# A decoder layer with 32 experts on one core: gate and up of the next expert ahead of each down, a direct gather for the first group, and one and a half weight units more loaded ahead

## What is computed

```python
def hier_moe(h, w_rg, b_rg, w_re, b_re, w_gate, w_up, w_down):
    ...
    lg = xf @ w_rg.astype(jnp.float32) + b_rg.astype(jnp.float32)
    pg = jax.nn.softmax(lg, axis=-1)
    g_star = jnp.argmax(lg, axis=-1)
    ...
    pe = jax.nn.softmax(le, axis=-1)
    top_p, top_i = lax.top_k(pe, TOP_K)
    w = p_group * top_p / jnp.sum(top_p, axis=-1, keepdims=True)
    e_idx = g_star[:, None].astype(jnp.int32) * EXPERTS_PER_GROUP + top_i.astype(jnp.int32)
    y = grouped_experts(x, e_idx, w.astype(x.dtype), w_gate, w_up, w_down)

# inside grouped_experts, for a block of tokens of one expert e:
        return (jax.nn.silu(xblk @ w_gate[e]) * (xblk @ w_up[e])) @ w_down[e]
```

## Time and profile before

| | us |
|---|---|
| median of 3 runs | 1452.62 (1452.39 to 1455.4) |
| the profiled execution, its own time | 1452.81 |
| its span in the profile | 1451.0 |
| TensorE busy | 1265.5 (87%) |
| VectorE, ScalarE, GpSimd busy | 474.1, 235.8, 53.5 |
| moved by DMA | 503.52 MB, 347 GB/s over the span |

### The profile page before, as it was taken

One profiled execution on the slowest core, in us unless ns is written; L12 is line 12 of the kernel. 1 busy time (PEld: TensorE's weight loads), 2 busy tenths in 40 slices (PEclk: granted clock), 3 DMA queues, 4 the chain that ended last, 5 costly groups with the idle time before them and its releaser, 6 DMA issues.

```text
span 1451.0 us, 20164 instructions
## 1 busy us (share of the span) xinstructions
PE 1265.5 (87%) x8401; PEld 655.4 (45%) x8401; DVE 474.1 (33%) x919; ACT 235.8 (16%) x475; POOL 53.5 (4%) x40
## 2 busy tenths in 40 slices
PE   9999999999999998886788797797787788779777
PEld 8888888888788852222222222122222222222222
DVE  4332138684111153422332232232232242233223
ACT  3111232312000041120011011111012002102101
POOL 0000003241000020000000000000000000000000
PEclk9999999999999999999899899999899999999999
DMA  9974433659396339999999999999999999999997
GB/s 342 349 232 169 135 131 137 221 192 334 113 347 246 136 144 429 428 435 429 433 433 429 431 434 433 433 429 434 431 432 431 433 433 433 429 433 425 429 428 308
DMA packets 97451, 503.52 MB, mean 347 GB/s; under 512 B 5150, under 2 KB 75478, under 8 KB 81030
## 3 DMA queue, kind: packets, MB, share of 16 engines
q1 hardware_dynamic: 89602, 494.33, 84.0%
q10 hardware_dynamic: 7508, 8.06, 1.6%
q0 software_dynamic: 304, 0.61, 0.2%
HBM read 496.42 MB, written 6.59 MB: 347 GB/s over the span
## 4 chain that ended last, share of the span: by engine, by line
PE 59%; DMA 35%; DVE 3%; ACT 1%; issue 1%; ACTq 0%; SPq 0%; DVEq 0%
PE bank L657 31%; DMA ring<-in_w_gate 30%; PE bank L932 8%; PE bank L959 5%; DMA ring<-in_w_up 5%; PE bank L871 3%; PE bank L977 2%; PE bank L974 1%; PE bank L942 1%; PE bank L990 1%; PE bank L984 1%; DVE bc L1717 1%; PE bank L949 1%; DVE xa L1702 1%; ACT bc L1298 1%
## 5 line engine op out<-in xcount | busy, mean ns | idle before, releaser
L657 PE MATMUL bank<-bc,ring 128*128 128x264 f32 x1536 | 350.8, 387 | 1.3 <-ACT cat L1086 1.3
L932 PE MATMUL bank<-ring,bc 128*32 128x512 f32 x2048 | 268.0, 647 | 94.7 <-DMA ring<-in_w_gate 62.2
L657 PEld LDWEIGHTS bank<-bc,ring 128*128 128x128 f32 x1536 | 288.2, 190 | 51.5 <-issue 2.3
L1702 DVE TENSOR_TENSOR xa<-xa,bank 128x512 f32<-128x512 f32 x224 | 138.9, 682 | 298.3 <-PE bank L977 298.3
L932 PEld LDWEIGHTS bank<-ring,bc 128*32 128x32 f32 x2048 | 61.1, 114 | 265.6 <-issue 240.8
L959 PE MATMUL bank<-ring,cat 128*32 128x512 f32 x1024 | 139.2, 692 | 13.9 <-DVE cat L1719 12.7
L657 PE MATMUL bank<-cat,ring 128*128 128x264 f32 x512 | 116.0, 387 | 0.0
L657 PEld LDWEIGHTS bank<-cat,ring 128*128 128x128 f32 x512 | 96.6, 190 | 19.0 <-issue 2.9
L1715 DVE COPY bc<-bank 128x512 f32<-128x512 f32 x32 | 22.1, 692 | 230.9 <-PE bank L932 230.9
L871 PE MATMUL bank<-cat,bc 128*32 128x512 f32 x512 | 65.0, 626 | 21.8 <-DVE xa L1702 20.1
L959 PEld LDWEIGHTS bank<-ring,cat 128*32 128x32 f32 x1024 | 36.1, 123 | 96.7 <-issue 95.0
(11 more groups left out here) (278 smaller groups left out, 932.0 us busy)
## 6 DMA issues: line engine op xcount, KB each, us to landing
ring<-in_w_gate SPq DMA_DIRECT2D x24, 4096.0 KB, 31.9
ring<-in_w_up SPq DMA_DIRECT2D x24, 4096.0 KB, 32.8
ring<-in_w_down SPq DMA_DIRECT2D x24, 4096.0 KB, 31.9
ring<-in_w_in SPq DMA_DIRECT2D x23, 2048.0 KB, 14.9
ring<-in_w_gate SPq DMA_DIRECT2D x16, 2048.0 KB, 24.1
ring<-in_w_up SPq DMA_DIRECT2D x15, 2048.0 KB, 32.0
ring<-in_w_down SPq DMA_DIRECT2D x15, 2048.0 KB, 25.3
ring<-in_w_out SPq DMA_DIRECT2D x8, 2048.0 KB, 16.6
```

The lines of the kernel that those rows point to most:

```text
L657: m = pe.matmul(bank[n % 3][:, 0:T], w[:, k, (i % TPU) * P:(i % TPU + 1) * P], src[:, k, :], start=n_k == 0, stop=n_k == KT - 1)
L932: m = pe.matmul(bank[b][c * C:(c + 1) * C, :], xeT[j % 2][:, k, :], w[:, x, :], start=i == 0 and x < 4, stop=i == 1 and x >= 4, skip_group ...
L1702: V.tensor_tensor(xa[:, t, cols], xa[:, t, cols], bank[to[n]][:, :], ALU.add).then_inc(mix_added, 1)
```

## The change

**Order of the loads** (`LOADS`): gate 0, up 0, gate 1, up 1, down 0, gate 2, up 2, down 1, gate 3, up 3, down 2, down 3. TensorE follows it: gate and up of expert j+1 are multiplied before down of expert j, and the mixes of an expert come one expert later. For the last two experts of a group tile 1 goes by `residual` and `mix_row`, so that VectorE has four adds fewer in a group.

**First group written out.** `experts(0, True)` stands ahead of the loop, which now runs over groups 1 to 7. The ninth unit (first half of down 0) goes to `xa[:, 0:2]` and half of the tenth (1 MiB) to 2048 columns of `bc`, both read in place by `down`; the other half of the tenth and the rest of the group take slots by `FIRST_SLOT` and wait for the unit in `FIRST_BEFORE`. `xa` is filled with the token rows after down 0 has read it: tile 0 by ScalarE, tile 1 by GpSimd.

**Direct gather.** `first_columns` multiplies 128 x 128 blocks of the rows (stationary) by `sel` (32 columns moving), 16 blocks by three token tiles, and so has the first expert's tokens in turned form without copy and transposes. The second half's tiles 1 and 2 come after the first gate unit. Twelve products of `keep_busy`, whose result nobody reads, stand ahead. VectorE runs the wide `select` before `first_gain(1)`.

```diff
+LOADS = [("g", 0), ("u", 0), ("g", 1), ("u", 1), ("d", 0), ("g", 2), ("u", 2), ("d", 1), ("g", 3), ("u", 3), ("d", 2), ("d", 3)]
+FIRST_BEFORE = {10: 0, 11: 2, 9: 1, 12: 3, 13: 4, 14: 5, 15: 6, 16: 10, 17: 9, 18: 11, 19: 12, 20: 13, 21: 14, 22: 15, 23: 7}
...
+            for m in range(SLOTS):
+                if m == 2:
+
+                    sp.wait_ge(o_ready, H + 1)
+                    sp.dma_start(spare, source(0, SLOTS)).then_inc(spare_in, 16)
+                used_wait(sp, NFRONT + m - SLOTS)
+                stream_unit(0, m, slot_of(NFRONT + m))
+
+            sp.wait_ge(y_T, NY)
+            sp.dma_start(spare_half, source(0, SLOTS + 1)[:, 0:UNIT // 2]).then_inc(spare_half_in, 16)
+            for m in FIRST_LOADS + tuple(range(16, UPG)):
+                s = slot_of(NFRONT + FIRST_SLOT[m])
+                if m == 10:
                     sp.wait_ge(half_used, 1)
...
+            keep_busy(12)
+            first_columns(0, (0, 1, 2))
+            first_columns(1, (0,))
...
+                    if j == 0:
+                        pe.wait_ge(row_moved, it * 4 + 2)
+                        unit_products(j, "g", 0)
+                        if first:
+                            first_columns(1, (1, 2))
+                        unit_products(j, "u", 0)
+                        pe.wait_ge(xe_ready, 2 * e + 2)
+                        unit_products(j, "g", 1)
+                        unit_products(j, "u", 1)
+                        next_rows(j)
...
+                    down(j - 1, 0)
+                    pe.wait_ge(hidden_ready, e + 1)
+                    down(j - 1, 1)
+                    turn_hidden(e)
+
+                e = it * EG + EG - 1
+                pe.wait_ge(ye_copied, e)
+                pe.wait_ge(gateT_copied, e)
+                for n in (0, 1, 3):
+                    mix_row(EG - 2, n)
+                pe.wait_ge(xe_ready, 2 * e + 4)
+                mix((0, EG - 2))
+                pe.wait_ge(act_ready, e + 1)
+                residual(2)
+                adds_done((0, EG - 2), -1)
+                mix_row(EG - 2, 2)
+                mix((2, EG - 2))
+                turn_gate(EG - 1)
+                down(EG - 1, 0)
+                down(EG - 1, 1)
...
             first_gain(0)
+            select(C, P, False)
             first_gain(1)
-            select(C, P, False)
```

More of the change, by code:

```diff
@@ L900, in first_rows @@
-                m.then_inc(gathered, 1)
-            first_rows(0)
-            first_rows(1)
+                        pe.wait_ge(h2_ready, (4, 8, NY)[t])
+                    for k in range(8 * half, 8 * half + 8):
+                        m_, c = divmod(k, 4)
+                        block = slice(c * 512 + m_ * P, c * 512 + m_ * P + P)
+                        if t < 2:
+                            lhs, rhs = h2[:, t, block], sel[:, t, 0:C]
+                        else:
+                            lhs, rhs = h2s[:, block], sel[0:NB, t, 0:C]
+                        m = pe.matmul(bank[(5, 7)[half]][:, k * C:(k + 1) * C], lhs, rhs,
+                                      start=t == 0 and k == 8 * half, stop=t == TT - 1,
+                                      skip_group_check=True)
@@ L1061, in _ @@
+            with pe.Fori(1, npass * NG) as it:
+                experts(it, False)
         @block.scalar
@@ L1259, in copy_rows @@
             def copy_rows(e):
-                act.wait_ge(gathered, e + 1)
-                act.wait_ge(xe_T, e)
+                act.wait_ge(gathered, e)
+                act.wait_ge(xe_T, e + 1)
                 A(xrow, bank[4][:, :], ACT.Copy).then_inc(xrow_copied, 1)
-            for half in range(2):
-                act.wait_ge(gathered, half + 1)
-                A(xrow[:, half * 256:half * 256 + 256], bank[(4, 6)[half]][:, 0:256], ACT.Copy).then_inc(xrow_copied, 1)
             act.wait_ge(stored[0], STORED[0] + 16)
@@ L1276, in _, with experts, copy_gate, copy_ye @@
                   h2s.rearrange("p (c m q) -> p q m c", c=4, m=4)[:, 32 * n:32 * n + 32], ACT.Copy).then_inc(xs_moved, 1)
+            A(nmax[:, 2:3], nmax[:, 0:1], ACT.Silu)
+            def experts(it, first):
+                def copy_gate(e, j):
+                    act.wait_ge(gate_T, e + 1)
+                    A(gateT, bank[GATE_BANK[j]][:, 0:TT * P].rearrange("p (t s) -> p t s", t=TT), ACT.Copy).then_inc(gateT_copied, 1)
+                def copy_ye(e):
+                    act.wait_ge(down_done, e + 1)
+                    A(ye, bank[2][:, :], ACT.Copy).then_inc(ye_copied, 1)
+                for j in range(EG):
+                    e = it * EG + j
+                    act.wait_ge(g_done, e + 1)
+                    A(g_sb, bank[0][:, :], ACT.Copy).then_inc(g_copied, 1)
+                    copy_rows(e + 1)
+                    if j >= 2:
+                        copy_gate(e - 1, j - 1)
+                    act.wait_ge(folded, e + 1)
+                    A(hidden, bank[3][0:C, :], ACT.Silu).then_inc(silu_done, 1)
+                    if j == 0:
+                        copy_gate(e, j)
+                        continue
+                    copy_ye(e - 1)
+                    if first and j == 1:
+                        for n in range(4):
+                            A(xa[:, 0, 512 * n:512 * n + 512].rearrange("p (q m c) -> p q m c", m=4, c=4),
+                              h2[:, 0, :].rearrange("p (c m q) -> p q m c", c=4, m=4)[:, 32 * n:32 * n + 32], ACT.Copy
+                              ).then_inc(x0_ready, 1)
+                copy_gate(it * EG + EG - 1, EG - 1)
+                copy_ye(it * EG + EG - 1)
+                for n in range(4):
+                    act.wait_ge(row_mixed, it * 4 + (n + 1))
+                    A(xa[:, 1, n * 512:(n + 1) * 512], bank[ROW_BANKS[n]][:, :], ACT.Copy).then_inc(row_moved, 1)
```

422 lines of the change are left out of this document (209 added, 213 removed).

## The result

The changed kernel takes 1459.1 us (7 runs, 1457.23 to 1462.53) against 1452.62 of the kernel before (7 runs by then, 1450.94 to 1455.4): ratio 1.0043, 95% interval 1.003 to 1.0056. It is slower by 6.5 us where I had forecast 1.2 less, and it lies outside my range of 1448.5 to 1455.5. The profiled execution took 1459.1, its span is 1457.3 (before: 1451.0).

The account below looks back on a forecast made before the run. The DMA stream bounds the second half. Early loads -7.3, start +2.3, gaps +1.8 and tail +1.8 sum to -1.4 us, from the profiled 1452.8 to 1451.4 us; range 1448.5 to 1455.5.

Parts of the forecast that it names:

- The likeliest case: The whole kernel: the forecast sum of -1.4 us, giving 1451.4 us, with a chance of 40%.
- slower: Direct gather: clock falls mid-gather and weight passes take twice as long at half clock, +5.4, 1458.2 us; chance 12%.
- half clock for the first up unit: First up unit, behind the gather's second piece: also at half clock, gap 3.5 us, sum +0.8, 1453.6 us; chance 18%.
- Units loaded ahead: Idle DMA time before the stream: one and a half units loaded early, 4.89 us each, worth -7.3 us.
- Start of the stream: TensorE's way to the first half gate unit: `half_used` at 540.3 in place of 538.03, +2.3 us.
- I take 0.113: Direct gather: each pass with 128-wide weights and 32 moving columns priced at 0.113 us.
- Gaps in the stream: Early loads waiting for TensorE: gaps of 1.8 and 0.4, 0.3 pauses, 0.5 ramp, less 1.2 lost before: +1.8 us.
- gather 3.6 us to 545.3, up unit 1.7 us at full clock: Behind the first gate unit: gather's second piece, then first up unit to 547.0, leaving a gap of 1.8 us.
- The first rival: Head of the stream: full clock from the turns to up 0, sum -3.1, 1449.7 us; chance 20%.
- The tail: After the last landing: down 3 ends at +3.3 us where it had been +1.2, a residual gone, +1.8 net.
- The loop: Groups in the loop: down one expert later, four VectorE adds fewer, a peeled group, 0 us.
- GpSimd and ScalarE: Copies of rows moved later: VectorE's selections relieved under the gather, new copies while four loads are queued, 0 us.

Follow-up runs that it names:

- e3: The changed kernel without the one and a half units loaded early, order and direct gather kept: 1466.28 us, ratio 1.0092 to the kernel before.
- e4: The changed kernel with the old row gather and no early loads, so only the new order and later copies remain: 1453.79 us, ratio 1.0006.
- e2: The changed kernel with the old row gather and no keep_busy, early loads and new order kept: 1446.88 us, ratio 0.9957 to the kernel before.
- e15: The new order alone (old gather, no early loads) with keep_busy(12) ahead of the gather: 1454.16 us, ratio 1.0013 to the kernel before.
- e13: The changed kernel with the old row gather in place of the direct one, keep_busy(12), early loads and new order kept: 1445.8 us, ratio 0.9958.
- e1: The changed kernel with each product of the direct gather moving its 32 columns four times over (128 columns): 1453.08 us, ratio 0.9999 to the kernel before.
- e6: The changed kernel with all 48 products of the gather's second half behind the first up unit: 1458.19 us, ratio 1.004 to the kernel before.
- e14: The kernel before with only keep_busy(12) added ahead of its gather: 1453.36 us, ratio 1.0011 to the kernel before.
- e10: e8 with 34 passes that nothing reads put ahead of the first gate unit: 1449.78 us, ratio 0.9978 to the kernel before.
- e12: The changed kernel without the twelve keep_busy products ahead of its gather: 1460.5 us, ratio 1.0053 to the kernel before.
- e7: The changed kernel with the edits of e1, e5 and e6 together: 1454.29 us, ratio 1.0009 to the kernel before.
- e5: The changed kernel with down 3's first unit moved ahead of TensorE's wait for VectorE's adds: 1459.65 us, ratio 1.0043 to the kernel before.
- e8: The changed kernel with the old row gather, no keep_busy, and down 3's first unit ahead of the adds: 1445.09 us, ratio 0.9945.

## Where the prediction failed

The likeliest case had 1451.4 and the kernel takes 1459.1. The mechanism that I named as *slower* (1458.2, 12%) is the one that came, with *half clock for the first up unit* on top; I had set it aside on a wrong reading of a row, told below.

**Units loaded ahead, -7.3: right.** 3.0 MB less in the stream, 7.2 us between e3 and the changed kernel, 6.9 between e4 and e2, 8.4 between e15 and e13. Down 0 read both of the early pieces without a wait (L1003 at 574.70 and 576.44).

**Start of the stream, +2.3: it was +4.5 to +4.9.** The failed step is "I take 0.113" for all 64 passes. Up to the fall it held (0.114). I had reasoned that the clock would be at half by the first gate unit, and still priced the passes ahead of it as at full clock, on the word of four weight loads in the earlier trace rows. Behind the fall, sixteen passes at 0.226 and sixteen at a mean of 0.146 cost 2.3 us more, and the gather began at 531.49 where I had 531.1: that is the 2.6 between 540.3 and 542.90. Those four loads were a poor measure, and the trace of the kernel before shows it. The same four take 0.55 us at a clock of 1.00 too (825.86), so something other than the weight load spaces them. The eight loads of a `mix`, of the same shape, do take longer at half clock: 0.31 us at 1.00 (809.24) and 0.52 at 0.50 (838.04). I had not compared either row at both clocks:

```profile
809.24 0.31 PEld L977 LDWEIGHTS bank<-bc 32*128 32x128 f32 x8 [1.24 <-issue]
825.86 0.55 PEld L949 LDWEIGHTS bank<-consts,bc 32*128 32x128 f32 x4
838.04 0.52 PEld L977 LDWEIGHTS bank<-bc 32*128 32x128 f32 x8 [1.67 <-issue]
```

What spaces the four I can't say. The formula of the Trainium skill ("TensorE: Matmul & The Clock Gate", LDWEIGHTS), which has the columns in it and not the clock, is contradicted by this trace in the same way: 0.114 us at 1.00 and 0.226 at 0.50 for the same shape.

**Gaps in the stream, +1.8: they were +5.7.** Two steps failed. "gather 3.6 us to 545.3, up unit 1.7 us at full clock" was 4.6 and 3.7 (the second piece lies from 543.94 to 548.58, unit 11 is issued at 552.28), behind a gate unit that itself ended 2.3 late (543.95 for 541.7). By the same working as in the prediction that makes the gap ahead of unit 11's data 4.5 us where I had 1.8. And the chain behind it, from the end of the first up unit to the load of unit 16, took 28.6 us (552.28 to 580.84) where I had 27.3: its seven units took about 13 and not 12.0, the first two of them in part at half clock. In e1, at full clock, the chain took 27.8. So the gap of 0.4 there became about 1.5 (560 to 600: 1.9 lost against 0.4). Beyond it the chain did gain on the loads, as I had it: +0.1 from 600 us on. e6 shows that the place of the passes hardly matters: moved about within that chain, they cost nearly the same.

The first rival failed in the same places. TensorE's lack of pauses did not hold the clock, and the full clock alone would not have made it right. At a full clock throughout I had 1449.7; e1 is that kernel, and it takes 1453.08. The start was at 541.0, 2.0 after the one before (I had +1.3), and the stream lost 1.8 more up to 600 (I had +1.1). With 0.8 more beyond 600 and in the taper, which I had not counted, and 1.7 at the end, which I had, that comes within 0.3 of its profiled execution of 1452.0.

**The tail, +1.8: right in size, and there was a taper above it.** The rest went from 13.0 to 14.8, in e15 too. That it came out so exactly is luck: my own terms add up to 1.6 (3.3 less 1.2, less 0.5 for the residual), and down 3 ended 3.9 us behind the last data where it had been 1.6, which is 2.3 more and not 2.1. The end of the stream came in more slowly by 1.0 (taper 3.4 against 2.4), which I had no term for; over the kernels it varies from 1.8 (e14) to 4.8 (e4) without an order that I could find, and its cause stays open.

**The loop, 0: right.** 1.4 lost before, 1.5 after, over 820 us.

**GpSimd and ScalarE, 0: right under the long gather, and only there.** I had let VectorE's relief from GpSimd's copies lie under the gather. With the short gather it shows: the 3.17 us of wait in e14 are gone in e15, and the 4.0 us between the two at the head of the stream are what that edit and the new order bring together. No run has one without the other.

The three parts of the change are now priced: early loads -7, order and copies about nothing (+0.2 in e4, +0.8 in e15: an end of +1.8, mostly paid back at the head), the direct gather +12 (e2; e13, with `keep_busy` kept, is 13.3 below the changed kernel). Without the gather, with `keep_busy` kept and one unit of down 3 moved, the kernel takes 1444.77 us, 0.57% under the kernel before.

## What to carry to other kernels

Price a product by the longer of its columns and its weight load, and both at the clock that its own kind of work leaves TensorE with: a product with 128-wide weights and 32 moving columns cost a full weight load here, and a row of them let the clock fall. Before you take a row at half clock as a price, find the same row at full clock: if both are equal, it measures something else. When all slots of a ring are full ahead of a stream, what the consumer spends before its first uses delays the stream by about as much (3.9 to 4.7 us for the pad of e10); the same pad three experts later cost 0.6, which is within the noise. When runs of a kernel spread over several microseconds, look for a stretch where the clock may or may not fall, hold the clock there, and only then compare medians for less than that.

## What was unexpected of the hardware

- A pass with 128 x 128 f32 weights took 0.114 us at a granted clock of 1.00 and 0.226 at 0.50; e12 has 64 passes of 0.226, half of them with 8-row weights. So the weight load follows the clock as the 512-column products do (16 passes in 1.92 us at 1.00, 3.64 at 0.50).
- The clock fell from 1.00 to 0.50 while TensorE was busy without a pause (5.01 of 5.01 us, then 4.40 of 4.40) with 32 moving columns a pass; with 128 columns a pass and the same weights it stayed at 1.00 in e1. In e7, with the same wide passes, it fell at 537.7, in a pause of 0.71 us right behind them.
- Where the clock fell and came back was not the same from one execution to the next. In the changed kernel it came back at 543.3 and was at half again from 546.7 to 553.6; in e5, whose code up to there is the same, it did not come back before 556.7. It fell at 532.2 in e8 and stayed at 1.00 in e2, again with the same code up to there.
- On VectorE, an instruction of 128 x 96 took 1.06 us while GpSimd copied rows (e14), 0.32 behind the last of these copies and in e2 without them.
